# Hybrid SSD / DeltaNet / PEER block on one core: V rows gathered by token and summed in quarters of TensorE

## The reference

```
scores -> top 16 of each half -> top 16 of the sums, for each of 8 heads: idx (token, 128), gates (token, 128)
act = gelu(einsum('td,tkd->tk', h, u_tab[idx]))       # 128 rows of U for each token
y   = einsum('tk,tkd->td', gates * act, v_tab[idx])    # 128 rows of V for each token
x   = x + y ; out = rmsnorm(x)
```

## Time and profile before

| | us |
|---|---|
| median of three runs (3827.57 to 3842.48) | 3833.96 |
| span of the profiled execution | 3815.1 |
| first gather issued | 663.9 |
| last gather issued | 3795.6 |

### The profile page before, as it was taken

How to read it: one execution, slowest core, us unless ns; L and a number is a source line. 1 busy time by engine, 2 the same in 40 slices (tenths; PEclk the granted TensorE clock), 3 DMA queues, 4 the chain that set the end, 5 groups by cost and what they waited for, 6 DMA issues and landing times. The chain is left out here.

```text
span 3815.1 us, 28982 instructions
## 1 busy us (share of the span) xinstructions
PE 2493.9 (65%) x7042; PEld 1238.9 (32%) x7042; DVE 2729.9 (72%) x5120; ACT 552.7 (14%) x1065; POOL 2477.6 (65%) x2125
## 2 busy tenths in 40 slices
PE   7999863566677667666766666566666667654166
PEld 4444452422243324322433233323332343211022
DVE  3332045989788878887788778787888788867844
ACT  2221010101111111111111111111111111111011
POOL 1100000687777778777787877787778777877776
PEclk9999986788787778788877888788878788877588
DMA  3334400899899999999999899999999999999998
GB/s 100 110 105 149 163 8 14 299 335 372 328 353 365 349 334 334 361 356 334 344 350 359 318 345 353 343 339 342 356 374 345 341 364 376 346 341 391 369 367 323
DMA packets 349585, 1159.17 MB, mean 304 GB/s; under 512 B 41216, under 2 KB 70800, under 8 KB 348432
## 3 DMA queue, kind: packets, MB, share of 16 engines
q0 software_dynamic: 301024, 1094.89, 78.0%
q1 hardware_dynamic: 46256, 58.69, 4.5%
q10 hardware_dynamic: 2176, 4.35, 0.3%
HBM read 1128.37 MB, written 29.43 MB: 303 GB/s over the span
## 5 line engine op out<-in xcount | busy, mean ns | idle before, releaser
L811 PE MATMUL y_psum<-ring,diag 128*128 128x512 f32 x1984 | 1216.2, 751 | 981.1 <-DMA ring<-in_peer_v_dram,at_row 669.6
L1136 DVE CUSTOM_DVE_ANT_0 ring<-ring,h_e 128x1024 f32<-128x1024 f32 x1024 | 1243.9, 1223 | 377.3 <-DMA ring<-in_peer_u_dram,at_row 367.2
L791 POOL DMA_INDIRECT ring<-in_peer_u_dram,at_row x986 | 1182.0, 1199 | 331.5 <-issue 278.9
L791 POOL DMA_INDIRECT ring<-in_peer_v_dram,at_row x704 | 835.3, 1187 | 217.2 <-issue 196.3
L811 PEld LDWEIGHTS y_psum<-ring,diag 128*128 128x128 f32 x1984 | 418.2, 231 | 1677.9 <-issue 878.0
L1158 DVE SCALAR_TENSOR_TENSOR y<-ring,coef,y 128x1024 f32<-128x1024 f32 x528 | 678.9, 1286 | 207.2 <-DMA ring<-in_peer_v_dram,at_tail 116.5
L791 POOL DMA_INDIRECT ring<-in_peer_v_dram,at_tail x320 | 366.0, 1144 | 119.1 <-issue 94.5
L995 ACT ACTIVATE diag<-ident_m,coef 128x128 f32<-128x128 f32 x496 | 190.6, 399 | 1130.1 <-PE y_psum L811 1014.3
L315 PE MATMUL proj<-hn_T,w_blk 128*128 128x512 f32 x640 | 280.0, 596 | 1.3 <-DVE hn_T L444 1.3
L944 PE MATMUL tile_psum<-w_q,arena 128*128 128x512 f32 x512 | 245.1, 641 | 8.8 <-ACT arena L1076 8.8
L775 POOL COPY at_head<-picks 128x10 uint32<-128x10 uint32 x8 | 4.2, 530 | 313.9 <-DVE picks L1377 312.6
(11 more groups left out here) (211 smaller groups left out, 2550.4 us busy)
## 6 DMA issues: line engine op xcount, KB each, us to landing
ring<-in_peer_u_dram,at_row POOLq DMA_INDIRECT x986, 6.3
ring<-in_peer_v_dram,at_row POOLq DMA_INDIRECT x704, 6.3
w_blk<-in_w_in_dram SPq DMA_DIRECT2D x20, 512.0 KB, 3.7
ch_scr<-post POOLq DMA_DIRECT2D x20, 512.0 KB, 2.9
tok_scr<-frames POOLq DMA_DIRECT2D x20, 512.0 KB, 3.8
w_q<-in_peer_w_q_dram SPq DMA_DIRECT2D x8, 1024.0 KB, 6.3
arena<-tok_scr SPq DMA_DIRECT2D x8, 768.0 KB, 9.1
ring<-in_peer_v_dram,at_tail POOLq DMA_INDIRECT x320, 6.3
```

Of the source, the lines that this page charges most:

```text
L791: pool.indirect_dma_start(ring[:, j], None, tables[kind], bass.IndirectOffsetOnAxis(ap=at, axis=0)).then_inc(filled[j], 16)
L811: last = nc.tensor.matmul(y_ps[:, half], diag[:, k % 2], ring[:, slot_of(item, e), half * BANK:(half + 1) * BANK], start=(k == 0), stop=(n ...
L1136: nc.vector.tensor_tensor_reduce(out=ring[:, j], in0=ring[:, j], in1=h2_e[:], scale=1.0, scalar=0.0, op0=ALU.mult, op1=ALU.add, accum_out= ...
```

## The change

1. **V by token.** The picks of a tile are transposed on TensorE (`picks_T`, copied to `at_T` for the next turn). A V gather now fetches, for one token, its 128 rows, one pick to a partition. Gather number n takes token n % 4 * 32 + n // 4, so four consecutive gathers are one token of each quarter of the tile.
2. **The sum on TensorE alone.** The coefficients are transposed too (`coef_T`). ScalarE lays them out in `spread`: for a token a block of 32 columns, of which one is the token's 128 coefficients and 31 are zero (item E: two small strided copies for 2 or 3 steps). `four` multiplies four tokens' blocks with their rows into the four 32-partition quarters of `y_ps`: 4 x 2 matmuls with 32 columns of weights and 512 moving columns. It starts only when all four have been gathered, and gives the slots free in its second half. The residual is added by a matmul with the identity (item R). L1158, L995 and L1163 are gone.
3. **Order.** Coefficients exist only when all 128 U of the tile are done. A turn is: 60 old V in pairs between 128 new U (the last 8 V behind the U), then 68 new V. The first turn has 196 gathers, seven have 256, the last has 60. Tokens 8 to 67 run in a loop on TensorE (three rounds of 20). On TensorE all new V stand behind the chain of the tile, on VectorE and ScalarE they lie beside the top-16 stages.
4. **h in PSUM.** `h_psum` (two banks) replaces `h2_e` as second operand of the U dots. The chain has four banks, with some steps moved and a few more waits; `row_of` uses transposes; some rows of the decays come from a transpose of `logs`.
5. One gelu for all 128 picks of a tile, and one product with the gates.

The order of gathers, and the ring slot that each waits for:

```diff
 def expert_sequence():
-    for n in range(PICKS):
-        seq.append(("U", n, 0))
-        while v < min(LAG, (n + 1) * 4 // 3 + 1):
-            seq.append(("V", TAIL + v, 1))
-            v += 1
-        if n >= LAG:
-            seq.append(("V", n - LAG, 0))
...
+    for v in range(FRONT, P - TAIL):
+        if v % 2 == 0:
+            to = P * (v + 2 - FRONT) // (BACK - TAIL)
+            seq += [("V", v, 1), ("V", v + 1, 1)]
+            for k in range(n, to):
+                seq.append(("U", k, 0))
...
+    seq += [("G", 0, 0)]
+    seq += [("V", v, 1) for v in range(P - TAIL, P)]
+    seq += [("C", 0, 0), ("E", 0, 0), ("F", 0, 1), ("R", 0, 0), ("E", 1, 0)]
+    for v in range(FRONT):
...
+        seq.append(("V", v, 0))
```

The work on one group of four tokens, and the U dot:

```diff
+            def four(v, back, e, r):
...
+                for half in range(2):
+                    for token in tokens:
+                        j, quad = slot_of(token, e), token[1] % QUADS
+                        if half == 0:
+                            pe.wait_ge(filled[j], 16 * (turn_of(token, e) + ROUND // SLOTS * r))
+                        last = nc.tensor.matmul(y_ps[quad * STEPS:(quad + 1) * STEPS, half], lines[:, quad, at:at + STEPS],
+                                                ring[:, j, half * BANK:(half + 1) * BANK],
+                                                start=False, stop=(step == STEPS - 1))
+                        if half:
+                            last.then_inc(used[j], 1)
...
-                    nc.vector.tensor_tensor_reduce(out=ring[:, j], in0=ring[:, j], in1=h2_e[:], scale=1.0, scalar=0.0,
+                    nc.vector.tensor_tensor_reduce(out=ring[:, j], in0=ring[:, j], in1=h_ps[:], scale=1.0, scalar=0.0,
                                                    op0=ALU.mult, op1=ALU.add, accum_out=dots[:, n:n + 1]).then_inc(used[j], 1)
...
-                    stt(out=y[:], in0=ring[:, j], scalar=coef[:, n:n + 1], in1=y[:],
-                        op0=ALU.mult, op1=ALU.add).then_inc(used[j], 1)
```

More of the change, by code:

```diff
@@ new lines @@
+STEPS = P // QUADS
+PITCH = 33
+ROUND_STEPS = 5
+ROUND = QUADS * ROUND_STEPS
+ROUNDS = 3
+LEAD_STEPS = 2
+LEAD = QUADS * LEAD_STEPS
+FRONT = LEAD + ROUNDS * ROUND
+BACK = P - FRONT
+TAIL = 8
+PRELUDE = 16
+assert BACK % SLOTS == 0 and ROUND % SLOTS == 0 and (STEPS - LEAD_STEPS) % ROUND_STEPS == 0
+WIDE, NARROW = 0, 1
+SPREAD_STEPS = (3, 2)
+SPREADS = [(NARROW, 0, LEAD_STEPS)]
+for first in range(LEAD_STEPS, STEPS, ROUND_STEPS):
+    SPREADS += [(WIDE, first, 3), (NARROW, first + 3, 2)]
+N_SPREADS = len(SPREADS)
@@ L895, in steps @@
                 for h in range(GDN_H):
[L896 removed]
+                    last = nc.tensor.matmul(heads(1)[:, h], k_in[:, h], Y[:, h], start=True, stop=True)
                 last.then_inc(s["w_ready"], 1)
+                for g in range(SSD_G):
+                    half = slice(g * SSD_R * SSD_P, (g + 1) * SSD_R * SSD_P)
+                    group = slice(g * SSD_R, (g + 1) * SSD_R)
+                    nc.tensor.matmul(bank[:, 3, half], C_T[:, g], S_ssd[:, group].rearrange("p h w -> p (h w)"),
+                                     start=True, stop=True)
                 pe.wait_ge(s["w_copied"], m + 1)
@@ L902, in steps @@
                 last.then_inc(s["v_new_ready"], 1)
+                pe.wait_ge(s["x_end_ready"], m + 1)
+                for g in range(SSD_G):
+                    half = slice(g * SSD_R * SSD_P, (g + 1) * SSD_R * SSD_P)
+                    group = slice(g * SSD_R, (g + 1) * SSD_R)
+                    last = nc.tensor.matmul(bank[:, 1, half], tok[:, TOK_B + g * P:TOK_B + (g + 1) * P],
+                                            x_end[:, group].rearrange("p h w -> p (h w)"), start=True, stop=True)
+                last.then_inc(s["ssd_out"], 1)
                 share()
```

365 lines of the change are left out of this document (183 added, 182 removed).

## The result

The changed kernel takes 4211.56 us (median of 4 runs, 4206.31 to 4215.72) where the kernel before, on the same chip, takes 3837.53 us (4 runs): a ratio of 1.099, 95% interval 1.096 to 1.103. It is slower, as forecast and inside the range, but by 374 us where 214 were forecast. The profiled execution has a span of 4204.7 us, against 4029 in the sum. The time alone would not name the cause: 4212 us lies above the 3920 to 4180 us that the prediction gives to its own case, and inside what it gives to rival A (4200 to 4550) and to C and D (4200 to 4370). The traces have to decide.

What follows compares the result with a forecast made beforehand. POOL's gather issue was taken to bound the kernel. POOL wins 430 us, the ring takes back 574 and smaller terms remain: 4029 us, plus 18.9 for the median, about 4050 us, 5.6% slower; 8-in-10 range 3800 to 4350.

Steps and rivals of the forecast that it cites:

- its own case: Whole kernel: POOL's gain is taken back by waits for V sums; 3920 to 4180 us, chance 0.60.
- rival A: V sums on TensorE: the four column quarters do not overlap, 6.9 us a group; 4480 us, chance 0.12 with partial overlap.
- C: Gathers: transfers are the limit, no gather below 1.40 us; about 4365 us, chance 0.09 together with D.
- D: U dots: the PSUM operand does not free POOL, up to half of 430 us stay; about 4250 us, 0.09 with C.
- the signs: Expected in the trace: POOL's mean issue near 1.0 us, some 90 waits of 5 to 7 us, 450 to 600 us total.
- POOL's issue as the pace of before: Kernel before: POOL issues gathers without a break, 1.49 us each, 3050 us for 2048; transfers are not at their limit.
- h in PSUM frees POOL: Gather issues beside VectorE: without two SBUF operands some 430 us of POOL's time go; bare step 1.245 us.
- The ring under groups of four: U parts: POOL waits L + d - 2 x 1.245 us for a group's slots, 6.4 us each, 7 x 82 = 574 us.
- L: Time from the issue of a group's last V gather to its landing, taken as 6.3 us.
- d: TensorE's time for one half of a group and the first matmul of the other, taken as 2.6 us.
- ring 82: Each full turn: POOL's waits for old V groups, 12 x 6.4 + 5.2 = 82 us.
- B: Same wait: landings shorten to 4.0 us when POOL stands still, wait 3.5 us; about 3790 us, chance 0.13.

Runs made afterwards that it cites:

- the sum of one: The changed kernel with the old V rows between the U gathers summed one at a time, new rows still four at a time: 3618.2 us, ratio 0.939.
- the pairs closer: The changed kernel with the two pairs of an old V group three U gathers apart and seven behind, not five and five: 4179.1 us, ratio 1.060.
- one quarter: The changed kernel with all four tokens' products of a group written to TensorE's first column quarter, except a turn's last group: 4685.2 us, ratio 1.189.
- the operand's test: whole groups with the U dot's second operand read from SBUF (a block of w_out) instead of h in PSUM: 4037.7 us, ratio 1.025.
- the sum of two: The changed kernel with old V rows summed two at a time, gather order untouched, new rows still four at a time: 3994.0 us, ratio 1.016.
- whole groups: The changed kernel with the four old V rows of a group gathered one behind the other instead of in pairs: 4047.8 us, ratio 1.028.

## Why the prediction was right, and what it sized wrong

The direction, the range and the mechanism are right: POOL stands in the U parts for sums of V rows, its issues beside U dots are short, and GB/s swings within a turn. The waits are more than the signs allowed, 123 of 837.9 us in total against some 90 of 450 to 600.

**POOL's issue as the pace of before: right.** Half the bytes leave the time at 1.004.

**h in PSUM frees POOL: right.** The mean issue is (965.5 + 582.0 + 452.1) / 2048 = 0.976 us, where before it was 1.187: 432 us less, 430 forecast. The step outside waits is 1.24 us (median; the mean, with the issues that L1361 and its like hold up, is 1.29). The bare step was right, and so was its price; the kernel with the operand in SBUF shows that the gain has no value while POOL waits anyway, and the sum of one, where it can be spent, shows a full turn of 367 us against 395 before (on the chip of the result).

**The ring under groups of four: the mechanism right, the single wait near.** 7.0 us against 6.4, with L = 6.7 and d = 2.8 for 6.3 and 2.6. Three doses bear it out: distance (4.0 to 4.7 us with the pairs closer, formula 3.9), landing (3.9 us with half the bytes, formula 4.0), and TensorE's time (7.5 to 9.3 us in one quarter). In the seventh turn, without a chain, the whole sum fits: 418.8 us, forecast 413. The first and last turns fit too: 310.8 and 79.5 against 316 and 83.

**The step that failed is the term "ring 82" for turns with a chain.** It took d to be 2.6 us wherever the group stands ("TensorE is in its chain when the rows land, too"). Six turns of 452.2 us in place of 422 are 181 us, and with the other turns (-5, +6, -4) that is the 176 us by which the span exceeds the sum. In the fifth turn (from 2332.8) the waits at the groups are 9.8, 11.3, 5.4, 6.2, 17.0 and 14.3 us, then seven of 6.6 to 7.2: together 112 us instead of 82. Nine of the thirteen are within 1.2 us of 6.4; the four at gathers 10, 23, 65 and 79 bring 4.6, 4.9, 10.6 and 7.9 us over it, 28 of the 30 missing. At the first of them it is L that was too small. TensorE stands idle there, and the group's third row, issued at 2342.01, lands at 2352.5: 10.5 us, where 6.3 were taken and where the same row of the seventh turn, which has no chain, took 6.4. The four loads of the next tile go out at 2337.6 to 2339.2 beside it; that they are the cause is likely, and not tested.

At the other three (23.4 of the 28 us) the rows have landed and TensorE is elsewhere: it reaches the sum only after steps of the chain that stand ahead of it in the program's order. I priced a group's wait as a latency and left out two things. One is this place in the order: in the timeline at 2462.63 TensorE runs two levels of the chain first, some 14 us, and VectorE is not what holds it up there. The other is what the wait itself does. With a group's first row held until its fourth is summed, only one gather can follow the fourth, so the U rows of VectorE come late, and with them its steps of the chain. The excerpt from 2469.91 on shows that: 8.69 us of TensorE idle ahead of the wait at gather 79, and every turn with a chain has such an idle time there, 8.6 to 9.0 us. Before gather 23 TensorE is idle for 14.4 to 15.3 us until a step of VectorE (L1242) that also stands behind U rows. Both show in the experiments: the two longest waits shrink from 20 and 18 us to 4 and 2 when a pair is held in place of a group, one goes from 17 to 20 down to 12 when TensorE takes the sum one share earlier, and half the bytes shorten neither of the two longest. How much of the 23 us is order and how much is late U rows was not separated.

**The rivals.** A is out: 16 records in 2.44 us, and on average 7.4 us for 12 when one quarter is used, against 4.4. (Its sum is also 6 us short: 68 and 60 V at 0.47 us more make the first turn 348 and the last 111 us, not 345 and 108.) The Trainium skill's 2.38 times for three column tiles ("TensorE: Matmul & The Clock Gate", Part 3) goes in the same direction: in the two groups shown, the ten records from 2591.41 on take 2.9 us and the ten from 4291.75 on 6.6 us, 2.3 times as long, with four quarters in float32 and parts of both at the lower clock (the granted clock was 0.62 and 0.65 there). B is out: landings stay at 6.3 to 7.4 us in the seventh turn, each behind a stall. C is out by the half rows and the step of 1.24 us, D by the operand's test.

**Left open:** why the "remote" waits come, and why on three of the chips only. What they are, the semaphores' events in the traces show. POOL goes on 0.75 us (median) after the event that frees its slot, in these waits as in the others. But the event itself is late: in an ordinary wait for TensorE it comes 0.05 to 0.06 us after the end of the matmul's record (medians), in the "remote" ones 4.3 us after it (the sum of two, 87 of the 97 waits) and 3.7 us (whole groups, 101 of 108). So POOL is not held up by itself, as theory B of the last experiment had it; TensorE's release reaches it late. ScalarE shows such waits behind TensorE too (L1129, 165.1 us in 12 with whole groups, none in the trace of the changed kernel shown above). Up to some third of the slots' events are missing from the traces of these chips (in the sum of two one slot has 126 of 201), so this rests on those that are there, and the cause stays open.

## What to carry to other kernels

When several transfers are consumed as one unit, price the unit by how long its first buffer is held: gathers between first and last, plus the landing, plus the consumer, against the depth of the ring. And ask how far the producer can still run ahead while it is held, since every engine that is fed through the same ring waits with it. Summing four rows at once saved TensorE busy time (1266.6 against 1376.2 us with one at a time, for 4096 records in both), which was not what the kernel waited for. Releasing each row by itself kept the gain of the rest of the change: 0.939 on its chip.

## What the hardware showed

- Time to land falls with the row here: 6.1 us for 4 KB a partition and 3.6 us for 2 KB (middle values, to the dot product that waited), while the issue stays at 0.94 to 0.95 us on POOL (medians). The kernel bound by issues gains nothing from half the bytes, the one bound by landings 5 to 6%.
- VectorE's dot product with one operand in PSUM leaves POOL's issue at 0.94 us; with both in SBUF it is 1.10 us on average beside the same work.
- The mean granted clock is 0.79 in the changed kernel and 0.87 with the sum of one, where TensorE stands idle for less time before its V records (590 us, not 914); a record of the V sum takes 730 and 674 ns. In the group behind the idle 6.63 us of the first timeline, the granted clock was 0.62 (2590 to 2594.5 us). The clock goes with TensorE's idle time rather than with POOL's waits: in one quarter POOL waits most and TensorE is busy longest, and the clock is 0.83.
- On three chips TensorE's release of a slot can reach POOL 4 us and more after the matmul's record ends (medians 3.7 and 4.3 us), where 0.05 to 0.06 us is usual (medians of the waits that the profile puts down to TensorE); on the two others no wait of POOL is of this kind.
- The kernel before took 3838 to 3940 us from chip to chip, a spread of 2.7%. The changed one took 4212 and 4379 us, 4% apart, on two chips where the kernel before differs by 2.5% (3838 and 3935). That a ring with little slack suffers more from a slower chip fits this, but two chips do not show it.
